# A dilated attention kernel: when its bias tables are loaded, how its rows lie in memory, and a 64-row second pass

## The reference

```
h = rmsnorm(x, g_attn_norm[l])
proj = h @ w_in[l]
q_a, k_a, v_a, c_q, c_kv, k_rope = jnp.split(proj, splits, axis=-1)
out_a = mixer_dilated(heads(q_a), heads(k_a), heads(v_a), rel_bias)
```

```
scores = jnp.einsum('bhrnqd,bhrnkd->bhrnqk', qblk, kb) * (dh ** -0.5)
scores = jnp.where(valid[None, None, None], scores + bias[None, :, None, None], NEG_INF)
m = jnp.max(scores, axis=-1, keepdims=True)
p = jnp.exp(scores - m)
l = jnp.sum(p, axis=-1, keepdims=True)
o = jnp.einsum('bhrnqk,bhrnkd->bhrnqd', p, vb) / l
```

## Time and profile before

| | us |
|---|---|
| median of 3 runs | 2899.49 |
| lowest and highest | 2894.95 and 2900.99 |
| the profiled execution: its own time | 2902.9 |
| its span in the profile | 2901.1 |

### The profile page before, as it was taken

How to read it: one execution, slowest core, us unless ns; L and a number is a source line. 1 busy time by engine, 2 the same in 40 slices (tenths; PEclk the granted TensorE clock), 3 DMA queues, 4 the chain that set the end, 5 groups by cost and what they waited for, 6 DMA issues and landing times. The chain is left out here.

```text
span 2901.1 us, 34464 instructions
## 1 busy us (share of the span) xinstructions
PE 2224.9 (77%) x12244; PEld 1836.5 (63%) x12244; DVE 1336.9 (46%) x2217; ACT 1022.6 (35%) x1809; POOL 534.2 (18%) x628
## 2 busy tenths in 40 slices
PE   6992975599969499996299997688397999464248
PEld 5881974499957266664178885577386888354137
DVE  4401652555544466664622112577464211375753
ACT  4400652355432155553321110345343111453331
POOL 0000000432011121221200004234130000464122
PEclk8995987799979599998599998788698999777669
DMA  5519965633044479983652213312444211221133
GB/s 198 214 46 193 209 141 182 164 95 79 12 164 138 153 306 366 361 337 149 239 185 77 80 48 98 89 44 51 139 138 160 83 70 51 83 66 32 47 138 102
DMA packets 223745, 400.74 MB, mean 138 GB/s; under 512 B 99168, under 2 KB 119008, under 8 KB 210672
## 3 DMA queue, kind: packets, MB, share of 16 engines
q1 hardware_dynamic: 175904, 300.50, 34.0%
q10 hardware_dynamic: 37664, 79.44, 7.2%
q0 software_dynamic: 10032, 18.90, 1.7%
HBM read 305.92 MB, written 110.66 MB: 144 GB/s over the span
## 5 line engine op out<-in xcount | busy, mean ns | idle before, releaser
L78 PE MATMUL pe_acc<-pe_w,hT 128*128 128x512 f32 x960 | 219.8, 392 | 8.7 <-DVE pe_w L197 8.7
L78 PEld LDWEIGHTS pe_acc<-pe_w,hT 128*128 128x128 f32 x960 | 181.5, 189 | 46.9 <-DVE pe_w L197 9.1
L78 PE MATMUL ex_gu<-hT,ex_xT 128*128 128x512 f32 x792 | 195.6, 403 | 0.8 <-DVE hT L1902 0.8
L1902 DVE TENSOR_TENSOR hT<-ex_raw,hT 128x2048 fp32r<-128x2048 f32 x66 | 150.9, 2287 | 87.9 <-ACT hT L1873 85.9
L78 PE MATMUL pg_acc<-hT,pg_w 128*128 128x512 f32 x768 | 176.1, 392 | 8.5 <-DVE pg_w L197 8.5
L78 PEld LDWEIGHTS ex_gu<-hT,ex_xT 128*128 128x128 f32 x792 | 148.5, 191 | 34.7 <-DVE hT L1902 1.2
L78 PEld LDWEIGHTS pg_acc<-hT,pg_w 128*128 128x128 f32 x768 | 144.8, 189 | 39.6 <-DVE pg_w L197 9.5
L1873 ACT ACTIVATE hT<-ex_raw 128x2048 fp32r<-128x2048 f32 x66 | 126.1, 1913 | 41.6 <-PEq L47 23.9
L262 DVE COPY pe_o<-pe_acc 128x512 f32<-128x512 f32 x28 | 19.4, 691 | 239.5 <-PE pe_acc L78 239.5
L1194 PE MATMUL ab_op<-ab_v,ab_pT 128*128 128x64 f32 x1024 | 121.3, 272 | 0.0
L1831 PE MATMUL ex_dn<-ex_wd,ex_hT 128*128 128x512 f32 x264 | 118.7, 593 | 0.8 <-ACT ex_hT L1867 0.8
(11 more groups left out here) (455 smaller groups left out, 5214.4 us busy)
## 6 DMA issues: line engine op xcount, KB each, us to landing
ex_raw<-in_w_gate SPq DMA_DIRECT2D x33, 1024.0 KB, 7.2
ex_raw<-in_w_up SPq DMA_DIRECT2D x33, 1024.0 KB, 11.2
ex_wd<-in_w_down SPq DMA_DIRECT2D x33, 1024.0 KB, 14.0
hT<-scr_qk SPq DMA_DIRECT2D x96, 256.0 KB, 7.7
scr_qk<-pa_parts ACTq DMA_DIRECT2D x32, 512.0 KB, 3.8
pe_raw<-in_even_w_in SPq DMA_DIRECT2D x6, 2048.0 KB, 7.9
pg_raw<-in_odd_w_in SPq DMA_DIRECT2D x5, 2048.0 KB, 8.7
e_e<-scr_y SPq DMA_DIRECT2D x16, 512.0 KB, 10.6
```

The costliest lines, as they stand in the source:

```text
L78: mm = pe.matmul(out, a(p, k), b(q, k), start=(k == 0 and i == 0), stop=(k == n - 1 and i == 2))
L1902: dve.tensor_tensor(split(s, LO)[:, :, g, :], raw[:, s % NW, g, :].rearrange("p (k n) -> p k n", k=8), split(s, HI)[:, :, g, :].bitcast(F3 ...
```

## The change

Bias tiles. A new class `Biases` owns the near and apart tiles (one copy each) across both stages. SP issues their two loads in the projections, behind the weights of the second chunk. In the attention POOL fills the edges of two extra tiles `aa_be` and copies the rest from the near tiles; VectorE uses the near tiles themselves for the six tiles in between.

Rows. Instead of `scr_qk` there are three scratch tensors. `q2` holds for each order and head the 64 high query rows twice, 128 rows of 1024; `ql` the low query rows once; `k2` for each head 64 high rows above 64 low ones. The projections write them: a query group leaves in six writes (for each order two of 64 rows x 2 x 512 and one of 128 x 512), a key group in four of 64 rows x 2 x 512. The attention loads a head in six: `k2` and `q2` as 128-row pieces and `ql` as 64 rows, for each order.

Scores. The first pass contracts 128 rows (twice the high query against high and low key), the second 64 (low query against high key). The product of the two low parts is left out.

V comes in two lots: the columns of heads 0 and 1 ahead of head 1's loads, the other six heads' behind them.

Memory. `pa_parts` is gone: the parts are a view of the output buffer `pa_o`. So both engines, before they empty the values' banks, wait until all query and key writes have landed. Around the two stages there is an outer `stage`, with an exit of its own.

```
-        parts = st.sb(name + "_parts", [P, 2, 2, 2, BANK], F32R) if cut else None
+        parts = obuf[:, :, :].rearrange("p (x o a) n -> p x o a n", x=2, o=2).bitcast(F32R)
...
+                    if g == 1 and also:
+                        also(sp)
...
+                    if cut and g > 0 and "split" in chunks[g - 1] and "split" not in ch:
+                        for u in range(2):
+                            act.wait_ge(cut_out[u], outs(cuts[g]))
...
-                                act.dma_start(ch["split"](o, j), parts[:, x % 2, o, :, :].bitcast(F32)).then_inc(cut_out[x % 2], 16)
+                                for dst, src in ch["split"](parts, x % 2, o, j):
+                                    act.dma_start(dst, src).then_inc(cut_out[x % 2], 16)
...
+def queries_to(twice, low):
+    def pairs(parts, x, o, j):
+        tt = slice((j % 2) * BANK, (j % 2 + 1) * BANK)
+        r0 = j // 2 * P
+        for b in range(2):
+            hi = parts[64 * b:64 * b + 64, x, o, HI, :].bitcast(F32)
+            yield twice[o, j // 2 * 2 + b].rearrange("(a d) s -> d a s", a=2)[:, :, tt], hi.unsqueeze(1).to_broadcast([64, 2, BANK])
+        yield low[o, r0:r0 + P, tt], parts[:, x, o, LO, :].bitcast(F32)
+    return pairs
+
+def keys_to(both):
+    def pairs(parts, x, o, j):
+        tt = slice((j % 2) * BANK, (j % 2 + 1) * BANK)
+        for b in range(2):
+            yield both[o, j // 2 * 2 + b].rearrange("(a d) s -> d a s", a=2)[:, :, tt], parts[64 * b:64 * b + 64, x, o, :, :].bitcast(F32)
+    return pairs
...
+class Biases:
+    def load(self, sp):
+        row = lambda at, w: bass.AP(self.table.tensor, at, [[1, P], [2 * BANK, 8], [1, w]])
+        sp.dma_start(self.near[:, :, :], row(0, QW)).then_inc(self.loaded, 16)
+        sp.dma_start(self.apart[:, :, :], row(BANK, QW + P)).then_inc(self.loaded, 16)
...
+                    for o, k in enumerate((kn[:, u, DV:DV + S], ka[:, u, :])):
+                        sp.dma_start(k.bitcast(F32), k_src[o, h]).then_inc(qk_in[u], 16)
+                        sp.dma_start(q2[:, u, o, :].bitcast(F32), q_src[o, h]).then_inc(qk_in[u], 16)
+                        sp.dma_start(ql[0:DV, u, o, :].bitcast(F32), ql_src[o, h * DV:(h + 1) * DV, :]).then_inc(qk_in[u], 16)
...
                 load_qk(0)
-                row = lambda at, w: bass.AP(table.tensor, at, [[1, P], [2 * BANK, HN], [1, w]])
-                sp.wait_ge(edges, 2)
...
                 sp.wait_ge(pads_in, 2)
+                load_v(0, 2 * DV, v0_in)
                 load_qk(1)
+                load_v(2 * DV, 512, v_in)
...
+                pool.wait_ge(bias.loaded, 32)
+                pool.tensor_copy(be[:, 0, :, 0:QW - DV], bias.near[:, :, 0:QW - DV]).then_inc(edges, 1)
+                pool.wait_ge(edges, 3)
+                pool.tensor_copy(be[:, 1, :, DV:], bias.near[:, :, DV:]).then_inc(edges, 1)
...
+                        for o in range(2):
+                            s = sps[T % 3][:, o * QW:(o + 1) * QW]
+                            pe.matmul(s, q2[:, u, o, ii], kk[o], start=True, stop=False)
+                            mm = pe.matmul(s, ql[0:DV, u, o, ii], kk[o][0:DV], start=False, stop=True)
```

More of the change, by code:

```diff
@@ L79, in product, with project @@
     return mm
-def project(nc, name, hT, nk, chunks, gain=None):
+def project(nc, name, hT, nk, chunks, gain=None, also=None):
     N = len(chunks)
@@ L107, in project, with outs @@
     nst = [[16 * kept[g][j] for j in range(groups(ch))] for g, ch in enumerate(chunks)]
+    def outs(x):
+        per = [ch["outs"] for ch in chunks if "split" in ch for _ in range(groups(ch))]
+        return 16 * sum(per[x % 2:x:2])
     def regroup(ap):
@@ L237, in _ @@
                     if cut:
-                        act.wait_ge(cut_out[u], 16 * sum(groups(c) for c in chunks if "split" in c))
+                        act.wait_ge(cut_out[u], outs(sum(groups(c) for c in chunks if "split" in c)))
             @block.vector
@@ L248, in _ @@
                         split_lo(dve, g + 1)
+                    if cut and g > 0 and "split" in chunks[g - 1] and "split" not in ch:
+                        for u in range(2):
+                            dve.wait_ge(cut_out[u], outs(cuts[g]))
                     for j in range(groups(ch)):
@@ L793, in dilated_attention @@
         W = S + P
[L794 to L798, removed]
+        q2, ql = (store[:, 4 * S * n:4 * S * (n + 1)].rearrange("p (u o s) -> p u o s", u=2, o=2) for n in range(2))
+        kn = store[:, 8 * S:8 * S + 2 * W].rearrange("p (u s) -> p u s", u=2)
+        ka = store[:, 12 * S:14 * S].rearrange("p (u s) -> p u s", u=2)
+        be = st.sb("aa_be", [P, 2, HN, QW])
         vn = st.sb("aa_vn", [P, NT + 1, 512])
@@ L928, in _ @@
                         if T == 0:
[L929 to L930 removed]
+                            dve.wait_ge(edges, 4)
+                            dve.wait_ge(bias.loaded, 32)
                         dve.wait_ge(s_done, T + 1)
@@ L933, in _ @@
                             dve.wait_ge(p_done, 2 * (T - 1))
-                        edge = 0 if i == 0 else 2 if i == T8 - 1 else 1
-                        bias = (bn[:, edge, h, :], ba[:, h, (i // 4) * P:(i // 4) * P + QW])
+                        near_bias = be[:, 0, h, :] if i == 0 else be[:, 1, h, :] if i == T8 - 1 else bias.near[:, h, :]
+                        tile_bias = (near_bias, bias.apart[:, h, (i // 4) * P:(i // 4) * P + QW])
                         for a in range(2):
-                            dve.tensor_tensor_reduce(out=sc[:, T % 2, a, :], in0=sps[T % 3][:, a * QW:(a + 1) * QW], in1=bias[a][:, ::-1],
+                            dve.tensor_tensor_reduce(out=sc[:, T % 2, a, :], in0=sps[T % 3][:, a * QW:(a + 1) * QW], in1=tile_bias[a][:, ::-1],
                                                      scale=1.0, scalar=-3e38, op0=ALU.add, op1=ALU.max,
```

92 lines of the change are left out of this document (46 added, 46 removed).

## The result

| | median us | lowest to highest | runs |
|---|---|---|---|
| before | 2900.24 | 2894.95 to 2907.96 | 4 |
| after | 3030.52 | 3023.92 to 3036.01 | 4 |

The ratio is 1.0446, 95% interval [1.0414, 1.0478]: the change costs some 130 us, where 59 less were forecast. Nothing in the range or among the rivals comes near it. The profiled execution of the changed kernel has a span of 3034.2 us, 133.1 more than before, at a mean granted clock of 0.828 (0.862 before).

The account below looks back on a forecast made before the run. It took the attention as bound by a 59 us start, then TensorE (14.5 us a head) with load waits and slow clock. -18.5 - 41.7 + 1 + 1 = -58.2 from 2902.9, less 3.4: 2841 us; range 2832 to 2858.

Parts of the forecast that it names:

- Scores: Attention's second score pass: contracting 64 rows instead of 128 costs 0, or 1 us either way.
- four periods of 3.1 us: Attention: slow clock after the idle start and three of four load waits; three periods (9.3 us) go, the start's stays.
- D: Rival, chance 0.04: the projections' 64-row writes go as slowly as the 768-byte bias pieces, +67 us, so 2908 us.
- Writes in the projections: Projections: more query and key write issues on ScalarE and 64-row pieces cost 0, with +8 us for an issue backlog.
- Rival B: Projections late, chance 0.11: backlogged issues hold ScalarE, TensorE waits at 174.8; +8 to +16 us, 2849 to 2857 us.
- Head loads: Attention: a head loads in 8.0 us, so waits inside the stage and three slow-clock periods go; -18.5 us.
- Next loads: Attention: head 2's loads, queued behind V, arrive on the edge; 0 to 5 us, taken as +1.
- Start: Start of the attention: earlier head, bias and V bring the first V product from 282.0 to 240.3; -41.7 us.
- one more stage exit: Exit of the added outer stage (semaphores cleared, barrier): below 3.4 us, taken as +1.

Follow-up runs that it names:

- e1: Changed kernel with the 64 low query rows padded with zeros, so the second score pass contracts 128 rows; 2865.94 us.
- e4: Changed kernel with the padded 128-row second pass in heads 0 to 3 and the 64-row pass in heads 4 to 7; 2889.49 us.
- e2: Kernel before with one edit: the second pass of each score contracts 64 rows instead of 128; 3053.85 us.
- e3: Changed kernel with a tile's passes in the order 128, 64, 64, 128 rows, two height changes instead of four; 2995.75 us.
- e10: Changed kernel with the 64-row second pass in heads 0 to 3 and the padded 128-row pass in heads 4 to 7; 2931.86 us.
- e5: Changed kernel with the second pass padded to 128 rows in head 0 only; four runs: 2902.78, 2989.55, 2993.35 and 2998.71 us.
- e6: e1 with SP issuing the regrouped (o = 1) query and key writes of the projections, ScalarE the others; 2851.42 us.
- e8: e1 with the bias loads put back behind head 0's loads at the start of the attention; 2883.42 us.
- e7: e6 with V in three lots, that of heads 4 to 7 loaded behind head 2's rows instead of ahead; 2851.49 us.
- e11: The same kernel as e5 run again, only head 0 padded to 128 rows in the changed kernel; 3002.72 us.

## Why the prediction was wrong

**Scores: the step that failed.** It put the 64-row second pass at 0, "or 1 us either way", by the mean duration of 64-row and 128-row matmuls (345 and 348 ns). That is the wrong column. A duration is not what a matmul costs in a stream; the step from one start to the next is, and it was there to be read, in the timeline of the retention stage in the kernel before:

```profile
1787.87 0.79 PE L2063 MATMUL re_o<-re_x,re_sc 128*128 128x128 f32 x2
1788.59 0.79 PE L2064 MATMUL re_o<-re_state,re_qkT 64*128 64x128 f32 x2
1789.32 0.79 PE L2063 MATMUL re_o<-re_x,re_sc 128*128 128x128 f32 x2
...
1791.62 1.11 PE L2039 MATMUL re_tp<-ident,re_rot 128*128 128x128 f32 x4
1792.52 0.64 PE L2042 MATMUL re_tp<-ident,re_dec 128*128 128x128 f32 x2
```

Four matmuls of one height running (the transposes at 1791.62) take 0.90 us, 0.22 each; where the height changes after every two, two take 0.72. One change of height thus costs 0.72 - 2 x 0.22 = 0.28 us by these rows, at a granted clock of 0.50, and the changed kernel has 256 of them in this stage. Measured, the pass costs 165 us (e1 against the changed kernel; in the stage alone 299.8 - 140.3 = 159.5): by e4's heads 46 for the 256 changes at full clock (0.18 us each; an estimate, no run had the pass in all heads at 1.00), and the rest, some 119, because the pass, begun at the lower level of the clock, never let it rise. The prediction had counted the slow clock as four periods of 3.1 us, one of which (the start) it kept, and took for granted that it would end. Here the pattern kept a low clock low for as long as it ran (290 us in the changed kernel, also in e2 and e3; 137 in e10) and left a high one high for up to 140 us (e4, e5), and in all thirteen traces the stage's first scores ran at 0.50, behind 15 to 21 us of idle TensorE.

This also means that no rival was near. The only one on the slower side, D, was about DMA.

**Writes in the projections: mis-sized.** It put 0, with +8 for a backlog; the measured price is +12 by the stages and 14.5 by e6. TensorE's waits in the projections of the changed kernel were for banks that VectorE had yet to empty (6.2 us, seven times from 133.7 to 179.2) and for converted weights (2.5, at 187.4). Its term "6 x 0.445" used the issue time of the old 128-row writes; the new ones took 0.83 us each in the slow round above. Of its two pictures, ScalarE's and the DMA's, it was ScalarE's. Rival B named the mechanism, and the size lies in its +8 to +16.

**Head loads: right.** Head loads of 8.0 us against 14.5 of TensorE: in e1 the stores of heads 1 to 6 follow each other at 14.48 us, with no wait for a load after head 2's. The -18.5 is not whole there, since one wait (5.6 us) and its slow clock remain.

**Next loads: right in place, wrong in size.** "On the edge: 0 to 5 us", taken as +1: head 2 came late by 5.56 us in e1 and 7.37 in e6, and the clock fell with it: from head 0's store to head 1's it is 23.2 us instead of 14.5, so the term was +9.

**Start: right.** Forecast from the first load: scores at +10.8, VectorE at +12.1. Measured +11.7 and +14.0, the latter with tiles slowed by changes of height; in e1 +11.1 and +12.5. The bias was in and POOL's copies took 1.46 us each, not 3.6. Undoing the early bias costs 17.5 us by the runs and 13.8 in the stage (e8). The term of 1 us for one more stage exit does not show: from the last head's store to the next stage's first load it is 6.8 us before and after.

**The size of what was right.** e1 is the change without the failed step: 2865.9, against 2841. The difference of 25 is the projections (12 to 14) and head 2 (8), and a few us that no trace places. e6 stands at 2851.4, with the first of these gone.

**The retention stage** is 12 us longer in the profiled execution of the changed kernel, but it took 58.6 to 82.8 us in the thirteen profiled executions of this study, with the same instructions in all: 58.6, 58.9 and 63.0 in e10, e6 and e1, 63.5 in the kernel before, 71.3, 75.1 and 82.8 in e7, e8 and e3. Its 75.4 in the changed kernel lies within that, so its 12 us need not be a price of the change. It alternates heights as well, and its length goes with the granted clock: the mean over the stage is 0.85 in the two shortest, 0.77 in those of 63 us, 0.64 in those of 75 and 0.56 in the longest. Each begins at 0.50, and in each the clock rose to 1.00 with the stage under way: 26 us from its first load in the kernel before, 53 in the changed one, 71 in e3. So alternating heights do not always keep a low clock low; what differs there (128 columns instead of 256, several matmuls of one height in a row) was not varied.

What stays open: the traces show that the clock stays low under these tiles with a 64-row pass and rises with the padded one; they don't show by what the chip decides. No run had 64-row passes without changes of height beside them, so which of the two holds the clock down is not shown; the price of the changes in time is. That e11's wait and the pattern together brought the clock down is read from one execution of each kind; a run with that wait put in or taken away was not made.

## What to carry to other kernels

- Keep one contraction height in a hot loop. A pass over 64 rows saved TensorE nothing here, and each change of height cost 0.18 us (2.4 GHz) to 0.3 us (1.2 GHz). Padding with zeros gave back all 165 us; putting the 64-row passes side by side gave back 35 of them (e3). To price a new shape, read the step between starts where that shape alternates with the old one, not a mean duration.
- A busy share of 100% says nothing of the clock. Ask of each stage at which level it starts, and whether its pattern can raise it: the same pattern costs some 46 us from a high start (by e4's heads) and 165 from a low one, and a kernel that sits between (e5) is two kernels, 90 us apart.
- Twice the pieces are twice the issues, each dearer. Count them on the engine that also has to empty the banks, and give half to an idle queue (14.5 us, e6).

## What the runs showed of the hardware that was not expected

- Changes between 128-row and 64-row matmuls cost 0.18 us each at a granted clock of 1.00 (e4) and 0.27 to 0.30 at 0.50 (e3, changed kernel). They are counted as busy.
- With four, or two, such changes in a tile the clock stayed at 0.50 for as long as the pattern lasted (290 us), TensorE shown as 100% busy; once the passes had 128 rows it was at 1.00 within 3 us (e10: first padded scores at 385.2, clock at 388.0).
- The retention stage, the same instructions in all, took 58.6 to 82.8 us, at a mean granted clock of 0.85 to 0.56.
- One kernel had two times, 2903 and 2990 to 3003 (e5, e11), told apart, in the two traces, by whether the clock stayed high after the pattern had begun.
- Writes of 64 rows x 2 x 512 elements took ScalarE 0.6 to 1.0 us each to issue; the former, of 128 rows, 0.445.
